# Unread products ahead of the projections and of the LayerNorm's column sums, in a hybrid conformer and attention step

## The reference

```python
h = rmsnorm(x); x = x + conv_mixer(h)      # layer 0
h = rmsnorm(x); x = x + attn(h)            # layer 1, differential attention
y = rmsnorm(x)
def conv_mixer(h, prev, ...):
    a, b, gate = split(h @ w_in, 3)        # 1024 -> 3 x 2048
    u = a * sigmoid(b)
    c = depthwise_conv31(concat(prev, u)) + dw_b
    c = silu(layernorm(c, ln_g, ln_b))
    return (c * silu(gate)) @ w_out        # 2048 -> 1024
def attn(h, ...):
    q, k, v, gate = split(h @ w_in)        # rope on q and k
    o = softmax(q1 k1) v - lam * softmax(q2 k2) v    # causal; samples also over 1024 cached keys
    return (rmsnorm(o) * (1 - lam_init) * silu(gate)) @ w_out
```

## Time and profile before

| | us |
|---|---|
| median of 3 runs | 2429.37 |
| lowest and highest | 2425.97, 2432.26 |
| the profiled execution, its time | 2426.89 |
| its span, first to last instruction | 2425.1 |
| PE busy | 2174.6 (90%) |
| DVE, ACT, POOL busy | 1182.8, 1028.4, 1343.2 |
| mean granted clock of TensorE | 0.913 |

### The profile page before, as it was taken

One profiled execution on the slowest core, in us unless ns is written; L12 is line 12 of the kernel. 1 busy time (PEld: TensorE's weight loads), 2 busy tenths in 40 slices (PEclk: granted clock), 3 DMA queues, 4 the chain that ended last, 5 costly groups with the idle time before them and its releaser, 6 DMA issues. The chain is left out here.

```text
span 2425.1 us, 38429 instructions
## 1 busy us (share of the span) xinstructions
PE 2174.6 (90%) x13067; PEld 1971.4 (81%) x13067; DVE 1182.8 (49%) x2195; ACT 1028.4 (42%) x1957; POOL 1343.2 (55%) x810
## 2 busy tenths in 40 slices
PE   5999999999349999999889988989898888898998
PEld 5999999999349998999889985766666666666998
DVE  4789889889883003222100006666666663346001
ACT  5555555555563112111221127766766773224111
POOL 3799999999744324433311227776676762225233
PEclk8999999999669999999999997877887887998999
DMA  7121222121224232222232331000010005882221
GB/s 247 45 71 52 61 61 61 44 70 52 88 72 124 62 115 71 79 70 92 76 97 89 105 114 45 18 29 17 18 36 9 10 1 175 258 266 67 62 79 72
DMA packets 182055, 192.69 MB, mean 79 GB/s; under 512 B 11434, under 2 KB 147059, under 8 KB 181331
## 3 DMA queue, kind: packets, MB, share of 16 engines
q1 hardware_dynamic: 181952, 191.48, 25.0%
HBM read 145.52 MB, written 47.63 MB: 80 GB/s over the span
## 5 line engine op out<-in xcount | busy, mean ns | idle before, releaser
L222 POOL TENSOR_TENSOR w_lo<-w_raw,w_hi 128x1024 fp32r<-128x1024 f32 x116 | 279.5, 2411 | 599.2 <-ACT w_hi L218 599.2
L242 PE MATMUL ps<-Hhi,w_hi 128*128 128x352 f32 x1704 | 560.1, 329 | 18.7 <-POOL w_lo L222 12.1
L242 PE MATMUL ps<-Hhi,w_lo 128*128 128x352 f32 x1704 | 549.9, 323 | 0.0
L242 PE MATMUL ps<-Hlo,w_hi 128*128 128x352 f32 x1704 | 548.9, 322 | 0.0
L788 DVE SCALAR_TENSOR_TENSOR ps<-U,dww,ps 128x512 f32<-128x512 f32 x608 | 403.0, 744 | 0.0
L218 ACT ACTIVATE w_hi<-w_raw 128x1024 fp32r<-128x1024 f32 x116 | 122.1, 1053 | 661.4 <-PE ps L242 244.4
L702 POOL TENSOR_TENSOR pool_acc<-pool_acc,prod 128x1024 f32<-128x1024 f32 x144 | 346.2, 2404 | 31.0 <-ACT prod L651 22.7
L242 PEld LDWEIGHTS ps<-Hhi,w_hi 128*128 128x128 f32 x1704 | 321.5, 189 | 28.4 <-POOL w_lo L222 18.8
L242 PEld LDWEIGHTS ps<-Hlo,w_hi 128*128 128x128 f32 x1704 | 322.4, 189 | 2.3 <-issue 0.2
L242 PEld LDWEIGHTS ps<-Hhi,w_lo 128*128 128x128 f32 x1704 | 321.4, 189 | 0.0
L651 ACT ACTIVATE prod<-U,dww 128x1024 f32<-128x1024 f32 x176 | 197.0, 1147 | 249.7 <-POOL pool_acc L702 143.2
(11 more groups left out here) (249 smaller groups left out, 4012.2 us busy)
## 6 DMA issues: line engine op xcount, KB each, us to landing
w_raw<-conv_w_in SPq DMA_DIRECT2D x48, 512.0 KB, 4.1
w_raw<-attn_w_in SPq DMA_DIRECT2D x40, 512.0 KB, 4.5
kpage<-cache_k SPq DMA_DIRECT2D x64, 256.0 KB, 3.0
vpage<-cache_v SPq DMA_DIRECT2D x64, 256.0 KB
res<-Y SPq DMA_DIRECT2D x2, 4224.0 KB, 16.8
gate<-sg SPq DMA_DIRECT2D x16, 528.0 KB, 4.0
sgl<-gate SPq DMA_DIRECT2D x16, 528.0 KB, 4.5
xres<-res SPq DMA_DIRECT2D x16, 528.0 KB, 3.9
```

Of the source, the lines that this page charges most:

```text
L222: pool.tensor_tensor(wlo[s][:, :, :], raw[s][:, :, :], whi[s][:, :, :].bitcast(F32), ALU.subtract).then_inc(w_lo, 1)
L242: mm = pe.matmul(ps[:, 3 * dst + c, 0:CH], w[:, k, :], r(k)[:, c * CH:(c + 1) * CH], start=start and k == 0 and w is whi[s] and r is rhs_h ...
```

## The change

Nine to twelve products are issued on PE whose results nobody reads. Each multiplies the first 128 x 128 tile of the rounded weights with 512 columns of the same buffer, into a PSUM bank that is free there. They stand in five places:

- ahead of the first projection unit of the conv block (9, bank 7), after the wait for its weights;
- ahead of the LayerNorm's column sums (12, bank 7), once five of the eight sums of squares are done;
- ahead of the first output projection (12, bank 0), once the second SiLU is done;
- ahead of the first attention unit (9, bank 7), after the wait for its weights;
- at the end of the samples' attention (10, bank 1), once the reciprocal of the small norm is done.

```diff
+        def idle_products(pe, bank, count):
+
+            for _ in range(count):
+                pe.matmul(ps[:, bank, :], whi[0][:, 0, :], whi[0][:, 0:4, :].rearrange("p k n -> p (k n)"),
+                          start=True, stop=True)
+
-        def unit_by_tile(pe, n, s, dst, nm):
+        def unit_by_tile(pe, n, s, dst, nm, ahead):
 
             pe.wait_ge(w_lo, n + 1)
+            idle_products(pe, 7, ahead)
             for k in range(KD):
...
-                        unit_by_tile(pe, n, e, e, norms[0])
+                        unit_by_tile(pe, n, e, e, norms[0], 9 if first and s == 0 else 0)
...
+                pe.wait_ge(w_lo, U_COUT + 1)
+                pe.wait_ge(lsum_done, JT // 2 - 3)
+                idle_products(pe, 7, 12)
                 pe.wait_ge(lsum_done, JT // 2)
                 column_sums(pe, lsum, 3).then_inc(lroot_step, 1)
...
                 pe.wait_ge(lrstd_ready, 1)
+                pe.wait_ge(silu_ready, 2)
+                idle_products(pe, 0, 12)
                 out_proj_pe(pe, outp[0], U_COUT, glo_of)
...
-                unit_by_tile(pe, U_ATT, 0, 0, norms[1])
+                unit_by_tile(pe, U_ATT, 0, 0, norms[1], 9)
...
                 pe.matmul(ps[:, 0, :], ones[:, :], dsq[:, :], start=True, stop=True).then_inc(smp_step, 1)
+                pe.wait_ge(smp_step, 4)
+                idle_products(pe, 1, 10)
```

## The result

| | before | after |
|---|---|---|
| median, 20 runs each on one chip, us | 2429.11 | 2433.32 |
| lowest and highest | 2425.97, 2433.86 | 2428.88, 2437.90 |
| profiled execution, its time | 2426.89 | 2435.57 |
| its span | 2425.1 | 2433.7 |
| mean granted clock | 0.913 | 0.917 |

The ratio is 1.0018, with a 95% interval of 1.0011 to 1.0025. The changed kernel is 4.2 us slower; that is inside the 0.3% called no change beforehand, and with 20 runs each it can still be told from zero. The forecast was 2430.9, in a range of 2424 to 2437.

What follows compares the result with a forecast made beforehand. PE was busy 90% of the span, so added work could give only clock. The profiled 2426.9 + 0 + 0 - 1.1 + 0 + 2.6 gave 2428.4, as a median 2430.9 us, range 2424 to 2437: no difference that shows.

Steps and rivals of the forecast that it cites:

- Rival 1: End of the samples' block: the barrier doesn't wait for the products, -2.4 in place of +2.6, 2425.9 us; chance 0.13.
- rival 4: Column sums: the clock doesn't rise for them, only the +2.6 at the barrier remains, 2432.0 us; chance 0.11.
- part 3: Twelve products ahead of the LayerNorm's column sums: part of the sums at the higher clock, -1.1 us, bounds 0 and -3.4.
- Price of a product: All five places: one added fp32r product of 512 columns takes 0.427 us at the lower clock.
- Rival 3: All five places: a product costs as plain float32, 1.87 us, so about +70, 2500 us; chance 0.04.
- Parts 1 and 2: Nine products ahead of the first conv and attention units: PE's gain waits for POOL, 0 each, bounds to -2.5 and -2.8.
- Part 4: Twelve products ahead of the first output projection: the saving is waited for at the 15th tile, 0, bounds 0 and -1.8.
- Part 5: Ten products at the samples' block's end: they hold the barrier, next block 2.6 us later, +2.6, bounds -2.4 and +3.1.
- rival 2: All five places: all starts are fast and all of it reaches the end, -12.9, 2416.5 us; chance 0.06.
- The fifth part's other half: Second output projection: the clock must rise within 4.3 us and hold 2.9 us; given nothing, first tiles slow as before.

Runs made afterwards that it cites:

- parts13: The changed kernel with only the products ahead of the first conv unit and ahead of the column sums: 2427.93 us, ratio 0.9985 to the kernel before.
- parts23: The changed kernel with only the products ahead of the first attention unit and ahead of the column sums: 2429.16 us, ratio 0.9987 to the kernel before.
- part3_only: The changed kernel with only the twelve products ahead of the column sums: 2426.14 us, ratio 0.9994 to the kernel before.
- no_part5: The changed kernel without the ten products at the end of the samples' attention: 2432.97 us, ratio 1.0016 to the kernel before.
- no_part5_again: no_part5 run unchanged a second time, in a later series: 2428.86 us, ratio 1.0010 to the kernel before.
- part3_early5: The changed kernel with only the column sums' twelve products and the samples' ten, these released one event earlier (smp_step 3): 2429.05 us, ratio 0.9996.
- part5_only: The changed kernel with only the ten products at the end of the samples' attention: 2431.47 us, ratio 1.0008 to the kernel before.
- bridge: part3_only plus ten products in the samples' block released one step earlier and six at the last block's start: 2427.72 us, ratio 1.0002.

## Why the prediction was right, and where it was not

Its mechanism held at the barrier, ahead of the column sums and in both `unit_by_tile` units, and nearly so at the output projection; its sum was right to within 3 us and lacked one term. That the measured time fell into the range says little by itself. The range, 2424 to 2437, held rivals 1 and 4 as well (2425.9 and 2432.0), and the measured 2433.3 is nearer to rival 4 than to the forecast of 2430.9. It is the profiles that tell them apart. There was luck in the sum too: a term of some +3 was left out, and part 3 was set 1.1 us too low for this profile, so the two errors took back part of one another.

- **Price of a product**: 0.427 us forecast, 4.18/9 = 0.46, 5.42/12 = 0.45 and 4.63/10 = 0.46 measured. Rival 3 is out.
- **Parts 1 and 2**: 0 forecast, 0 measured. The first unit started 0.25 us later, where 0 to 0.1 was forecast, and had the higher clock 1.0 us after that; the attention unit had it from the start, because the group kept up a clock that had risen without it. Both wait for POOL's remainders again, as the earlier trace rows said; parts13 and parts23 lie no higher than part3_only beyond their intervals.
- **Part 3**: -1.1 forecast, -2.2 measured in this profile (column sums -1.8, the steps up to the scaling -0.4). Here the clock came late, at 689.68, 0.2 us before the twelve ended, and held through all of the column sums, whereas I had them get 1.4 to 2.25 us of it. What I described does occur: in parts13, parts23, no_part5 and no_part5_again the clock rose before the twelve had ended and fell during the column sums. From the last sum of squares to the scaling it is 6.8 to 8.0 us over the eleven profiles with the group, against 8.98, so the gain is 1.0 to 2.2 us, and the forecast lies at its low end. Rival 4 (no rise) didn't occur in any of them: from their release the column sums take 2.2 to 2.8 us in ten, 3.0 in parts23, against 4.05.
- **Part 4**: 0 forecast, -0.02 us at the 15th tile in the changed kernel. From the first product to the first sum with the residual (47.45) it gains 0.6 us on part3_only (48.0), but nothing on before (47.46). I had read PE and the elementwise chain as level from one profile, in which the clock rose after only 3.5 us; where it takes 5.6 us or more PE is the later of the two, and the group is worth 0.5 to 0.8 us.
- **Part 5**: +2.6 forecast, +2.94 measured; the difference is the price of ten products. One event earlier the barrier isn't held (5.33, 5.34, 5.34 us in three kernels), and in part3_early5 the clock falls before it is used. Rival 1 (the barrier doesn't wait) is out, and with it rival 2, which needed a gain at every start.
- **Missing**: the samples' block, some +3 us (182.3 to 183.1 against 179.3 where the clock was no worse; 185.8 in the changed kernel's own profile). I had followed each added product only through its own stage, and its work, not its length as code. -2.2 + 2.9 + 3 = +3.7, against 4.2 measured (2.7 to 6.1).

The fifth part's other half was the clock. In the changed kernel it rose 4.4 to 5.3 us after three groups' starts and 5.3 after a projection's, and not at all in the 4.63 us of the last group. The ten of part3_early5 did raise it, after 2.9 us; it fell 2.4 us after they ended. The Trainium skill (TensorE: Matmul & The Clock Gate, "HAM oscillation — how this bites in real kernels") says that a wait between bursts takes the clock down again, and the trace agrees. The queue of 64 in the table at the head of that page of the Trainium skill does not free the barrier: the block opened at 2217.50, 0.25 us after the last of the ten, and in part5_only too (2211.37 after 2211.12).

Why the whole is small: of the five starts only one, the column sums, has nothing slower beside it. At the others PE's gain meets POOL (parts 1 and 2, and most of part 4) or is never made (part 5). As to a better version: of the six kernels that keep group 3, don't hold the barrier and haven't all of groups 1 to 4, five have ratios of 0.9985 to 0.9996 and the bridge 1.0002. So some 0.1% can be had from group 3, whose own stage gives 1.0 to 2.2 us; which of the six is best can't be told.

## What to carry to other kernels

Unread products ahead of a burst pay only where PE's burst is on the chain that ends last, where they end before what they wait for is due, and where no barrier or gap stands between them and the burst; here that was one place in five, and a second (group 4) now and then. Put them behind an event early enough that the engine is free at the block's end: an engine's queued work holds the barrier even if nobody reads it. And compare every stage of the two profiles, not only the edited ones; a stage that the edit doesn't touch gave as much as one that it does. Added instructions also move the packets of the kind "instruction" behind them, and the list of DMA queues shows where they come to lie.

## What was not expected of the hardware

- The column sums (18 products of one column, 2.17 us) kept the higher clock that came too late for the twelve products ahead of them: it rose at 689.68, 0.2 us before they ended, and fell at 693.08.
- With a gap of 0.74 us between two bursts (bridge: 4.63 us, gap, 2.90 us) the rise came 9.3 us after the start. Behind the wide groups 1, 3 and 4 of all profiles it came 3.4 to 6.1 us after theirs. It is one profile, and that the gap did it is not shown.
- The stretch between the output projection's end and its norm's spread, which no edit touches, took 7.3 to 9.4 us over the profiles (its two groups of column sums took 3.27 and 3.98 us before, 2.14 and 3.35 after, by the clock), and prompt attention 546.9 to 553.7, for a reason that no run shows. One profile against another says nothing below some 2 us in the one and 6 us in the other; the samples' block can be read only because nine and five profiles fall into two groups.
- One issue of a load on SP took 1.0 to 1.2 us longer at the start of the samples' block in exactly those kernels with 42 products added on another engine ahead of it, even where 30 of them were narrow. In exactly those a packet of the kind "instruction" (queue 8, 0.9 to 1.1 us) ran beside it. That the one delays the other is not shown.
